# Rounded RG-LRU gates, a channel tile for sliding-span values, and output tiles begun inside two attentions

## What is computed

```python
# first block, RG-LRU branch (width 1536, 16 blocks of 96)
xl = causal_dwconv(lru_x, lru_conv_w, lru_conv_b)              # 4 taps
r = sigmoid(einsum('bsni,nij->bsnj', xl_blocks, w_a) + b_a)    # block-diagonal, 96 x 96
i = sigmoid(einsum('bsni,nij->bsnj', xl_blocks, w_x) + b_x)
log_a = -8 * r * softplus(-lam); a = exp(log_a)
u = sqrt(-expm1(2 * log_a)) * (i * xl)
h[t] = a[t] * h[t-1] + u[t]
y_lru = h * silu(lru_gate)
# second block, one layer
h = rmsnorm(x, pre_norm); x = x + rmsnorm(branch(h), post_norm)
# S5: u, z = h @ w_in; complex diagonal scan, y = gelu(Cs + du); y * sigmoid(y @ w_glu + b) * silu(z) @ w_out
# sliding span: 16 query heads, 2 key/value heads of 64, window 128, bias and sinks: (o * silu(z)) @ w_out
# MLA: 16 heads, latent queries (768) and keys/values (256), rope, causal: (o * silu(z)) @ w_out
# SGU: u, v = gelu(h @ w_in), v layer-normed, mixed along chunks of 128: (u * s * silu(z)) @ w_out
```

## Time and profile before

| | |
|---|---|
| median of three runs | 1879.34 us |
| the profiled execution | 1878.01 us |
| its span | 1876.3 us |
| TensorE busy | 1853.1 us, 99% |
| VectorE busy | 1256.6 us, 67% |
| ScalarE busy | 906.7 us, 48% |
| GpSimd busy | 478.3 us, 25% |

### The profile page before, as it was taken

One profiled execution on the slowest core, in us unless ns is written; L12 is line 12 of the kernel. 1 busy time (PEld: TensorE's weight loads), 2 busy tenths in 40 slices (PEclk: granted clock), 3 DMA queues, 4 the chain that ended last, 5 costly groups with the idle time before them and its releaser, 6 DMA issues.

```text
span 1876.3 us, 26257 instructions
## 1 busy us (share of the span) xinstructions
PE 1853.1 (99%) x10210; PEld 1515.3 (81%) x10210; DVE 1256.6 (67%) x1917; ACT 906.7 (48%) x1568; POOL 478.3 (25%) x530
## 2 busy tenths in 40 slices
PE   9999999999999999999999999999999999999998
PEld 7887787888567888988899887888787876698887
DVE  8998876548569337666467855778669477648364
ACT  6648777312288214542343354537545565545333
POOL 1781110575258504024114621020001300000000
PEclk9999999999999999999999999999999999999999
DMA  5336442334222535445627934511123411123221
GB/s 185 103 120 198 144 145 76 125 148 154 90 87 93 157 112 171 166 144 159 202 79 202 227 91 110 126 68 57 57 103 110 136 50 35 46 90 135 99 70 68
DMA packets 71739, 222.17 MB, mean 118 GB/s; under 512 B 17200, under 2 KB 17888, under 8 KB 70720
## 3 DMA queue, kind: packets, MB, share of 16 engines
q1 hardware_dynamic: 43920, 157.03, 25.1%
q0 software_dynamic: 24240, 55.79, 10.6%
q10 hardware_dynamic: 3456, 7.67, 1.4%
HBM read 203.23 MB, written 14.81 MB: 116 GB/s over the span
## 4 chain that ended last, share of the span: by engine, by line
PE 84%; DVE 11%; ACT 3%; issue 1%; DMA 0%; DVEq 0%; POOL 0%; ACTq 0%; POOLq 0%
PE bank L489 24%; PE bank L490 23%; PE bank L491 23%; DVE ring_low L451 3%; DVE sq L716 2%; PE bank L3884 1%; PE bank L2198 1%; PE bank L3917 1%; PE bank L1113 1%; PE bank L2205 1%; DVE lru_x L2299 1%; PE bank L3274 1%; DVE x L1717 1%; PE bank L3656 1%; ACT ring_high L446 1%
## 5 line engine op out<-in xcount | busy, mean ns | idle before, releaser
L446 ACT ACTIVATE ring_high<-ring 128x1024 fp32r<-128x1024 f32 x283 | 297.2, 1057 | 524.3 <-PE bank L491 523.6
L451 DVE TENSOR_TENSOR ring_low<-ring,ring_high 128x1024 fp32r<-128x1024 f32 x283 | 389.1, 1385 | 231.6 <-ACT ring_high L446 231.0
L489 PE MATMUL bank<-h_high,ring_high 128*128 128x512 f32 (+1 forms) x1276 | 500.9, 393 | 3.2 <-DVE ring_low L451 2.1
L491 PE MATMUL bank<-h_high,ring_low 128*128 128x512 f32 (+1 forms) x1276 | 489.7, 384 | 0.0
L490 PE MATMUL bank<-h_low,ring_high 128*128 128x512 f32 (+1 forms) x1276 | 489.6, 384 | 0.0
L489 PEld LDWEIGHTS bank<-h_high,ring_high 128*128 128x128 f32 x1276 | 239.9, 188 | 63.9 <-issue 14.2
L490 PEld LDWEIGHTS bank<-h_low,ring_high 128*128 128x128 f32 x1276 | 240.1, 188 | 48.2 <-issue 2.9
L491 PEld LDWEIGHTS bank<-h_high,ring_low 128*128 128x128 f32 x1276 | 239.9, 188 | 47.6
L489 PE MATMUL bank<-gated_high,ring_high 128*128 128x512 f32 (+1 forms) x240 | 85.5, 356 | 1.1 <-DVE gated_low L3486 1.1
L490 PE MATMUL bank<-gated_low,ring_high 128*128 128x512 f32 (+1 forms) x240 | 83.3, 347 | 0.0
L491 PE MATMUL bank<-gated_high,ring_low 128*128 128x512 f32 (+1 forms) x240 | 83.3, 347 | 0.0
(11 more groups left out here) (584 smaller groups left out, 3799.3 us busy)
## 6 DMA issues: line engine op xcount, KB each, us to landing
ring<-slabs SPq DMA_DIRECT2D x287, 512.0 KB, 3.3
acs_rows<-acs_rows POOLq DMA_DIRECT2D x16, 512.0 KB, 4.6
s_outputs<-s_ca POOLq DMA_DIRECT2D x4, 1152.0 KB, 5.0
exp_acs<-acs_rows POOLq DMA_DIRECT2D x16, 256.0 KB, 10.0
s_b<-s_br POOLq DMA_DIRECT2D x8, 512.0 KB, 4.5
s_rows<-s_powers POOLq DMA_DIRECT2D x16, 256.0 KB, 7.4
s_inputs<-s_w POOLq DMA_DIRECT2D x8, 512.0 KB, 3.3
s_ck<-s_outputs POOLq DMA_DIRECT2D x1, 4096.0 KB, 24.5
```

The lines of the kernel that those rows point to most:

```text
L446: act.activation(self.ring_high[:, self.splits_before[s] % AHEAD, :], self.ring[:, s % RING, :], ACT.Copy)\
L451: dve.tensor_tensor(self.ring_low[:, s % RING, :], self.ring[:, s % RING, :], self.ring_high[:, self.splits_before[s] % AHEAD, :].bitcast( ...
L489: pe.matmul(out, w[0], x[0], start=start, stop=False, **flags)
L491: return pe.matmul(out, w[1], x[0], start=False, stop=stop, **flags)
```

## The change

- `lru_gates` is no longer plain: its slabs are split, the conv outputs `lru_x` are split as well (`L.XP`), and each product is three rounded passes. A corner is now stored in a full block of 128 columns with zeros (two blocks for each gate and three tiles), and the corner passes alternate between two products on different rows of the array. A new semaphore, `half_in`, orders the second half of them. The first conv tap goes to ACT, the chain for `SPA` goes ahead of the x stage.
- In the g stage the groups have four tiles, the gate product goes from POOL to DVE, and the high and low of the result go to ACT and DVE in the gate tiles that follow.
- In `stage_xbc` the slab lows behind tiles 21 and 22 move behind the conv taps. In `stage_sgu` the last low moves behind the last root product.
- In S5 the last z tile is made in two pieces (six products, then two behind a y), and the inputs of tile i+2 are loaded at z of tile i.
- In `gated_output` the first two tiles are interleaved (products 0 to 5 of both, then 6 and 7 of both), and both attentions begin the first tile within their last turn: 2 + 3 products in `stage_swa`, 3 + 2 in `stage_mla`.
- Sliding span: values come as a second channel tile next to the keys and are transposed on TensorE (four transposes); the entry takes no sums by token. Scores and z tiles are ordered anew at the start.
- MLA: the second key tile goes ahead of the first scores; the scores of each even turn are divided by one product of a z tile.

```diff
-PLAIN = ("lru_gates",)
+PLAIN = ()
@@ lru_corners
-    return [(a + 1, slice(0, 64), a, slice(96, 128), slice(96, 128)), (a + 1, slice(64, 128), a + 2, slice(0, 32), slice(0, 32)),
-            (a, slice(96, 128), a + 1, slice(0, 64), slice(32, 96)), (a + 2, slice(0, 32), a + 1, slice(64, 128), slice(32, 96))]
+    return [[(a + 1, slice(0, 64), a, slice(96, 128)), (a + 1, slice(64, 128), a + 2, slice(0, 32))],
+            [(a, slice(96, 128), a + 1, slice(0, 64)), (a + 2, slice(0, 32), a + 1, slice(64, 128))]]
@@ gemm
-    def gemm(self, pe, tile, moving, seen, n=T, ready=None):
+    def gemm(self, pe, tile, moving, seen, n=T, ready=None, ks=None):
...
@@ stage_xbc, DVE
-                if i in split_at:
+                if i in split_at and split_at[i] < 21:
...
-            C.split_low(dve, tiles[-1][0])
+            for u, _ in tiles[21:]:
+                C.split_low(dve, u)
@@ stage_lru, x stage, ACT
+            for i, (u, _) in enumerate(x_tiles):
+                C.split_high(act, u)
+                C.full(act, u)
+                act.activation(L.XL[:, i, :], C.bank[u.b][:], ACT.Identity, scale=C.col("lru_conv_w", 36 + i),
+                               bias=C.col("lru_conv_b", i)).then_inc(tapped.sem, 1)
+                if i > 0:
+                    high(i - 1)
@@ stage_lru, gates, TensorE
-                        pe.matmul(C.bank[u.b][:], C.block(s, i), L.XL[:, m, :], start=True, stop=True)
+                        C.product(pe, C.bank[u.b][:], C.block(s, i), (L.XP.high[m], L.XP.low[m]), True, True)
...
-                for gate, n in ((0, 0), (0, 1), (1, 0), (1, 1), (0, 2), (1, 3), (1, 2), (0, 3)):
...
-                    mm = pe.matmul(C.bank[u.b][c, :], C.block(s, i)[r, at], L.XL[r, k, :], start=False, stop=True, skip_group_check=True)
+                for pairs in (((0, 1, 0), (1, 1, 1)), ((0, 0, 0), (0, 0, 1)), ((1, 0, 0), (1, 0, 1)), ((0, 1, 1), (1, 1, 0))):
+                    if pairs[0] == (0, 1, 1):
+                        pe.wait_ge(half_in.sem, half_in.at(2 * t + 1))
+                    for weight, moving in ((0, L.XP.high), (0, L.XP.low), (1, L.XP.high)):
+                        for gate, kind, n in pairs:
...
+                            mm = pe.matmul(C.bank[u.b][:], C.block(s, i)[weight][r, :], moving[k][r, :],
+                                           start=False, stop=True, skip_group_check=True)
@@ stage_lru, g stage
-    NB, BUFS = 2, 4
+    NB, BUFS = 4, 4
...
+                    x = L.XL[:, m, :]
+                    dve.tensor_tensor(x, x, L.G[:, m % BUFS, :], ALU.mult).then_inc(gused.sem, 1)
             for m in range(KD):
                 gates.on_dve(dve, m)
+                for k in range(2 * m, min(2 * m + 2, KL)):
+                    dve.wait_ge(highs.sem, highs.at(k))
+                    dve.tensor_tensor(L.OUT.low[:, k, :], L.XL[:, k, :], L.OUT.high[:, k, :].bitcast(F32), ALU.subtract)\
+                        .then_inc(out.sem, 1)
@@ stage_s5_scan
+        if s + 1 == NB - 1:
+            order.append(("z end", s + 1))
...
+                    C.gemm(pe, z[i], C.H.tiles(KD), seen, ks=range(KD if i < NB - 1 else 6))
+                elif kind == "z end":
+                    C.gemm(pe, z[i], C.H.tiles(KD), seen, ks=range(6, KD))
@@ gated_output
+            C.gemm(pe, tiles[0], gate.parts.tiles(KD), seen, ready=split_ready, ks=range(done, 6))
+            C.gemm(pe, tiles[1], gate.parts.tiles(KD), seen, ks=range(6))
+            C.gemm(pe, tiles[0], gate.parts.tiles(KD), seen, ready=split_ready, ks=range(6, KD))
+            C.gemm(pe, tiles[1], gate.parts.tiles(KD), seen, ks=range(6, KD))
@@ stage_swa, TensorE
             scores(0)
+            C.gemm(pe, zb[0], C.H.tiles(KD), seen, ks=range(3))
             scores(1)
-            for j in range(2):
-                C.gemm(pe, zb[j], C.H.tiles(KD), seen)
+            C.gemm(pe, zb[0], C.H.tiles(KD), seen, ks=range(3, KD))
+            C.read(pe, L.kv_tiles[1][0])
+            C.open(pe, vt)
+            for t in range(TC):
+                mm = pe.transpose(C.bank[vt.b][:, t * P:(t + 1) * P], L.K[:, 1, t * P:(t + 1) * P], C.ident[:])
...
+            C.gemm(pe, zb[1], C.H.tiles(KD), seen)
...
+                if j == NJ - 1:
+                    begin_output(range(2))
...
+                if j == NJ - 1:
+                    begin_output(range(2, 5))
@@ branch_swa
-    L.k_tile = stage_gemm(C, 1, hk, entry.times_root(L.K), "vector", side=Side(pool=root_queries))[0][0]
-    L.v_uses = stage_tokmajor(C, 1, hk, lambda half, t: L.V[:, t, :], TC, factor=entry.token_root)
+    L.kv_tiles = stage_gemm(C, 2, hk, entry.times_root(L.K), "vector", side=Side(pool=root_queries))
@@ stage_mla, TensorE
             C.gemm(pe, kb[0], L.KV.tiles(2), seen)
+            C.gemm(pe, kb[1], L.KV.tiles(2), seen)
             scores(0)
             scores(1)
-            C.gemm(pe, kb[1], L.KV.tiles(2), seen)
...
+                if h == H - 1:
+                    begin_output(range(3))
...
+                if h + 2 < H and h % 2 == 0:
+                    scores(h + 2, range(3))
+                    C.gemm(pe, zb[h // 2 + 1], C.H.tiles(KD), seen, ks=range(1))
+                    scores(h + 2, range(3, TC))
+                    C.gemm(pe, zb[h // 2 + 1], C.H.tiles(KD), seen, ks=range(1, KD))
...
+                if h == H - 1:
+                    begin_output(range(3, 5))
@@ stage_sgu, DVE
-                C.split_low(dve, u)
+                if i < KD - 1:
+                    C.split_low(dve, u)
                 C.full(dve, u)
                 times_root(dve, i, C.bank[u.b]).then_inc(C.bank_read[u.b], 1)
+                if i == KD - 1:
+                    C.split_low(dve, u)
```

More of the change, by code:

```diff
@@ L2280, in _, with ratios @@
             ln = C.vchain.link
-            def ratios(b):
-                for m in range(b, b + NB):
+            def ratios(*ms):
+                for m in ms:
                     t, q = C.sq[:, m % BUFS, :], C.root[:, m % BUFS, :]
@@ L2335, in _, with inputs_used @@
                 gates.on_act(act, m)
-    return gates, lambda eng, k: eng.wait_ge(out.sem, out.at(k))
+                for k in range(2 * m, min(2 * m + 2, KL)):
+                    act.wait_ge(gused.sem, gused.at(k))
+                    act.activation(L.OUT.high[:, k, :], L.XL[:, k, :], ACT.Copy).then_inc(highs.sem, 1)
+    def inputs_used(eng):
+        eng.wait_ge(ix.sem, ix.at(KL - 1))
+        eng.wait_ge(scanned.sem, scanned.at(KL - 1))
+        eng.wait_ge(gused.sem, gused.at(KL - 1))
+    return gates, lambda eng, k: eng.wait_ge(out.sem, out.at(k)), inputs_used
 class MemoryAttention:
@@ L3387, in _ @@
                 if kind == "z":
+                    if i + 2 < NB:
+                        C.full(act, vb[i])
+                        loads.load_inputs(act, i + 2)
+                    if i < NB - 1:
+                        C.split_high(act, z[i][0])
+                elif kind == "z end":
                     C.split_high(act, z[i][0])
@@ L3391, in _ @@
                 elif kind == "v":
-                    if i + 1 < NB and i >= 1:
-                        C.full(act, vb[i - 1])
-                        loads.load_inputs(act, i + 1)
+                    if i == 1:
+                        C.full(act, vb[0])
+                        loads.load_inputs(act, 2)
                     if 3 <= i + 1 < NB:
@@ L3487, in low_on_dve, with gated_output @@
             .then_inc(self.low.sem, 1)
-def gated_output(C, gate, Z, layer, side=Side()):
+def gated_output(C, gate, Z, layer, side=Side(), begun=None, done=0):
     C.pinned = (7,)
-    tiles = [C.take_tile(KD) for _ in range(KD - 2)]
+    tiles = ([] if begun is None else [begun]) + [C.take_tile(KD) for _ in range(KD - 2 - (begun is not None))]
     ends = [[C.take_bank() for _ in range(2)] for _ in HALVES]
@@ L3767, in _ @@
             C.split_high(act, zb[0][0])
+            C.full(act, vt)
+            act.activation(L.V[:].rearrange("p t c -> p (t c)"), C.bank[vt.b][:], ACT.Copy).then_inc(C.bank_read[vt.b], 1)
             exps(1)
@@ L3785, in _ @@
             gate.high_on_act(act, NJ - 1)
+    return begun
 def swa_places(C):
@@ L3878, in _, with begin_output, scores @@
             seen = set()
-            def scores(h):
+            def begin_output(ks):
+                C.gemm(pe, begun, gate.parts.tiles(KD), seen, ready=lambda k: pe.wait_ge(gate.low.sem, gate.low.at(k)), ks=ks)
+            def scores(h, rows=range(TC)):
                 pe.wait_ge(kt_.sem, kt_.at(K0 + h))
-                for i, u in enumerate(sb[h]):
+                for i in rows:
+                    u = sb[h][i]
                     C.open(pe, u)
```

231 lines of the change are left out of this document (138 added, 93 removed).

## The result

The changed kernel takes 1858.76 us (median of four runs, 1858.56 to 1858.82), the kernel before beside it 1878.78: a ratio of 0.9893 [0.9876, 0.9911]. Twenty us are gone; the forecast was 1853.7, with a range from 1848.5 to 1865.0. The direction and most terms were right, and 5 us were not. The small bounds around the forecast, 1850 to 1857, would have missed it by 1.8; it lies in the range because room for rival (a) had been taken in.

What follows compares the result with a forecast made beforehand. TensorE, busy 1853.1 of 1876.3 us, was taken to bound the kernel, so only its work and gaps count. Terms summed to -25.9, banks gave +0.3: 1878.0 - 25.6 = 1852.4, plus 1.3 is 1853.7 us; range 1848.5 to 1865.0.

Steps and rivals of the forecast that it cites:

- small bounds around the forecast: Conv +1.1, S5 and MLA, gates -1.7 around the forecast time: 1850 to 1857 us.
- rival (a): RG-LRU gates: rounded corner passes run singly, stage 40.0 against 29.1 us, total 1864.6 or 1862.7; chance 0.11.
- g stage: Stage after the gates: less POOL work and fewer ACT table loads remove TensorE's waits, -2.6 us (0 to -2.7).
- MLA's end: End of MLA: 3 + 2 output products cover the 1.4 us wait for the last scores' exponentials, -2.0 us.
- bank term of the sum: Begun output tiles keep a bank longer: 0 to +0.5 us, taken as +0.3.
- Gates: RG-LRU gates: rounded passes with paired corners, 7.28 us a round including 0.47 for shape changes, -7.0 us.
- S5's scan: S5, last z tile: the 0.9 us DMA wait goes but VectorE's chain is late next, -0.1 (0 to -1.1).
- Conv stage: End of the conv stage (xbc): two slab lows of 1.13 us move behind the taps, -2.2 us.
- (b): g stage: moved waits come back because DVE keeps its dear prices, +4 to +14, 1858 to 1868 us; chance 0.07.
- (c): Shape changes cost nothing and S5's wait goes wholly: 1851.0, or 1849 if odd heads' waits gain too; chance 0.15.
- (d): Slower than before: groups of four in the g stage make ACT and DVE take turns, +57, 1911 us; chance 0.03.
- (e): Whole kernel: gaps moved and not closed, only removed work counts, -12.4, 1866.9 us; chance 0.03.

## Why the prediction was right, and where it was not

- **What bounds it, and by what prices.** Right. A rounded pass at 0.227 and refill of 0.16 behind each wait carried the sliding span (6.3 of 6.6; its end 2.1 of 2.1), S5's output, MLA's start and SGU's end to within 0.4 us each. The g stage was right in size; which of its reasons were needed is open in part.
- **MLA's end.** The step that failed is "3 + 2 products stand in between: -2.0". It counted cover and did not ask which bank the begun tile gets; the bank term of the sum, 0 to +0.5, was taken from the nearest row and was wrong by its place. With the bank taken earlier the step gives what it said: the table's +2.5 less the 4.6 of the traces is -2.1. The clock's fall, 1.55 of the loss in the profiled execution, was in no bound.
- **Gates.** The mechanism was right (pairs, a price for changes); the term for changes was mis-sized, 0.47 a round for what measures 0.87, since a round has one change more and two of the others cost more than they did in the narrower corners. "About as often as before" was a miscount: four changes and not three.
- **S5's scan.** The step said that VectorE's chain would be late next, and gave it the range 0 to -1.1. It is late by more than the DMA was, 0.7, and dividing the tile itself costs 0.3 to 0.4: +1.1 against the kernel before. The end of the range on the other side was missing.
- **Conv stage.** -2.2 took a wait for a queue; 0.9 of it was the last tile's own chain.
- **Rivals.** (a) fell by the pairs' starts, (b) by VectorE's prices in the changed kernel (lows 1.34, ratios 0.69) and no wait in its g stage, (c) by the price of a change, (d) and (e) by the table. The four misses add to 8.1 us one way and the small differences of the other rows of the table to 1.9 the other: 6.2, as the profiled execution's 1858.56 against the sum's 1852.4. Of this 1.1 is hidden in the median, since I had added 1.3 between the profiled execution and the median and the changed kernel's (1858.56 and 1858.76) differ by 0.2.
- **Signs of being wrong, and luck.** The prediction called a new wait of over 1 us in any of these stages wrong, and there are two, 2.8 in MLA and 1.6 in S5. Of the waits that were to go, 0.8 stays at the conv stage's end; a round of the gates takes 7.68 and not 7.3. The time is in the range by bounds that were put there for other reasons: 1865.0 stands for single corner passes, which do not occur, and the term for banks had room for 0.5 and not for 4.6.

## What to carry to other kernels

A product that is put ahead to cover a wait also takes a buffer: look up who last used the one that its turn falls on, and where that reader stands in its own queue, before counting cover. When a queue's work is moved behind the critical item, the gain ends where the item's own input arrives. And an order that needs several shapes of the array pays 0.2 us for every change, so count changes per round and put independent work, not a wait, between two uses of the same bank.

## What the runs showed of the hardware

After TensorE had stood for 3 us between dense stretches, its granted clock fell to 0.56 over the next 3.8 us in some executions, with passes 0.427 us apart, and stayed at 1.00 in others of nearly the same kernel; a gap of 1.66 us left it alone. Two rounded matmuls of 512 columns on different rows of the array start together and take the time of one. A change of the array's shape costs 0.20 us with rounded passes, half before it and half behind, and the same with plain ones on tiles of 128 columns; with corners of 32 and 64 columns it was 0.12 and 0.14. VectorE's scan of 128x512 takes 1.22 us alone and 2.20 beside a GpSimd product of the same size.
